# Three passages of a two-block network: where VectorE's low parts and a modulation unit stand, and how many fillers TensorE runs

## The reference, cut to what matters

```python
mod = cond @ ada_w[layer] + ada_b[layer]        # shift1, scale1, gate1, shift2, scale2, gate2
hn = rmsnorm(x, norm1_w[layer]) * (1 + scale1) + shift1
y = mlstm_mixer(hn, ...)  # layer 0;  hgrn2_mixer(hn, ...) in layer 1
x = x + gate1 * y
hn = rmsnorm(x, norm2_w[layer]) * (1 + scale2) + shift2
y = swiglu(hn, ...)       # layer 0;  moe_swiglu(hn, ...) in layer 1, 8 experts, top 2
x = x + gate2 * y
```

## Time and profile before

| | |
|---|---|
| median of three runs | 1492.36 us (1489.75 to 1493.78) |
| profiled execution, its span | 1492.0 us |
| TensorE busy | 1435.4 us, 96% |
| VectorE busy | 1129.3 us, 76% |
| ScalarE busy | 773.8 us, 52% |
| mean granted TensorE clock | 0.989 of full |
| HBM read | 343.65 MB, 231 GB/s over the span |

### The profile page before, as it was taken

The page is one execution under the profiler, slowest core; times in us unless marked ns, Lnnn a source line. Parts: engine busy times, 40 slices in busy tenths (PEclk is TensorE's granted clock), DMA queues, the critical chain, the costliest instruction groups (busy, mean ns, idle before and its releaser), DMA issues.

```text
span 1492.0 us, 21141 instructions
## 1 busy us (share of the span) xinstructions
PE 1435.4 (96%) x8403; PEld 1235.9 (83%) x8403; DVE 1129.3 (76%) x1244; ACT 773.8 (52%) x829; POOL 4.1 (0%) x7
## 2 busy tenths in 40 slices
PE   3998989999999999999999999999999999999999
PEld 3976889799798788878888888787887787899997
DVE  5898578766779866798989889988886767655544
ACT  1535333333455463777777767776565443533332
POOL 0000000000000000000000000000000000000000
PEclk9999899999999999999999999999999999999999
DMA  8877278876865463799999999984554345345652
GB/s 314 274 266 270 64 246 275 301 254 222 271 219 185 148 239 115 255 341 334 333 342 313 362 337 330 352 304 141 175 171 162 113 129 181 114 156 197 198 162 105
DMA packets 198431, 345.83 MB, mean 232 GB/s; under 512 B 11632, under 2 KB 90064, under 8 KB 193232
## 3 DMA queue, kind: packets, MB, share of 16 engines
q1 hardware_dynamic: 190320, 338.71, 66.8%
q10 hardware_dynamic: 8032, 6.01, 1.3%
HBM read 343.65 MB, written 1.05 MB: 231 GB/s over the span
## 4 chain that ended last, share of the span: by engine, by line
PE 51%; DVE 6%; issue 2%; ACT 2%; DVEq 0%; ACTq 0%
PE ps L1313 15%; PE ps L1315 15%; PE ps L1314 15%; DVE wlo L2104 3%; ACT whi L634 1%; PE ps L1372 1%; PE ps L1959 1%; PE ps L1999 1%; DVE HL L2955 0%; PE ps L1982 0%; DVE acc L2945 0%; PE ps L1510 0%; PE ps L1519 0%; PE ps L1518 0%; PE ps L1432 0%
## 5 line engine op out<-in xcount | busy, mean ns | idle before, releaser
L2104 DVE TENSOR_TENSOR wlo<-raw,whi 128x2048 fp32r<-128x2048 f32 (+2 forms) x220 | 480.2, 2193 | 157.3 <-ACT whi L634 151.9
L634 ACT ACTIVATE whi<-raw 128x2048 fp32r<-128x2048 f32 (+2 forms) x220 | 403.8, 1837 | 359.1 <-PE ps L1315 232.8
L1313 PE MATMUL ps<-whi,AH 128*128 128x512 f32 (+1 forms) x816 | 321.4, 394 | 3.7 <-DVE wlo L2104 2.2
L1315 PE MATMUL ps<-whi,AL 128*128 128x512 f32 (+1 forms) x816 | 312.4, 383 | 0.0
L1314 PE MATMUL ps<-wlo,AH 128*128 128x512 f32 (+1 forms) x816 | 312.2, 383 | 0.0
L1313 PE MATMUL ps<-AH,whi 128*128 128x256 f32 x896 | 256.4, 286 | 3.4 <-DVEq L2210 1.4
L1314 PE MATMUL ps<-AL,whi 128*128 128x256 f32 x896 | 254.6, 284 | 0.0
L1315 PE MATMUL ps<-AH,wlo 128*128 128x256 f32 x896 | 254.5, 284 | 0.0
L1313 PEld LDWEIGHTS ps<-whi,AH 128*128 128x128 f32 x816 | 154.0, 189 | 40.9 <-DVE wlo L2104 11.0
L1313 PEld LDWEIGHTS ps<-AH,whi 128*128 128x128 f32 x896 | 173.1, 193 | 5.9 <-issue 2.9
L1315 PEld LDWEIGHTS ps<-whi,AL 128*128 128x128 f32 x816 | 153.7, 188 | 28.2
(11 more groups left out here) (345 smaller groups left out, 1452.1 us busy)
## 6 DMA issues: line engine op xcount, KB each, us to landing
raw<-in_ada_w SPq DMA_DIRECT2D x48, 1024.0 KB, 5.5
raw<-in_w_in SPq DMA_DIRECT2D x26, 1024.0 KB, 5.2
raw<-in_moe_w_up SPq DMA_DIRECT2D x24, 1024.0 KB, 7.0
raw<-in_h_w_in SPq DMA_DIRECT2D x16, 1024.0 KB, 5.8
raw<-in_moe_w_gate SPq DMA_DIRECT2D x16, 1024.0 KB, 7.3
raw<-in_moe_w_down SPq DMA_DIRECT2D x16, 1024.0 KB, 6.5
acc<-in_moe_w_down SPq DMA_DIRECT2D x16, 1024.0 KB, 7.7
raw<-in_m_w_in SPq DMA_DIRECT2D x12, 1024.0 KB, 6.0
```

The lines of the kernel that those rows point to most:

```text
L634: act.activation(whi[:, h, 0:n], raw_at[s][:, 0:n], ACT.Copy).then_inc(w_hi, 1)
L1313: pe.matmul(o, sh, mh, start=first, stop=False)
L1315: return pe.matmul(o, sl, mh, start=False, stop=last)
L2104: dve.tensor_tensor(wlo[:, h, 0:n], raw_at[s][:, 0:n], whi[:, h, 0:n].bitcast(fp), ALU.subtract)\
```

## The change

At passage 1 the first of the next stage's two low parts and the modulation unit go ahead of residual 0, and the second low part goes behind the features. At passage 3 the first low part goes ahead of residual 0, the second behind three small preparations of the router (the last a `memset`), ahead of the wait for the router's product. At passage 2 residual 0 goes ahead of the down product's last low part (only in the second group, `early`), one of the next stage's two low parts stays ahead of residual 1, and one goes behind the features. ScalarE's second high part goes ahead of `first_squares` at passages 1 and 3; at passage 2 the first goes ahead of it and the second stays behind it. Fillers ahead of the transposes: 12 to 11, 16 to 10 and 20 to 11; ahead of the experts: 11 to 3. The order of the loads that SP issues is the same.

```diff
             for j in range(LEAD):
                 hi(w)
                 skip_first(j)
-                if j == 0:
-                    first_squares(0)
+            first_squares(0)
             second_squares(0)
...
+            hi(w)
             first_squares(1)
-            his(w, LEAD)
+            hi(w)
             second_squares(1)
...
-            hi(w)
+            his(w, LEAD)
             first_squares(2)
-            hi(w)
             second_squares(2)
...
-            transposes(w, 12)
+            transposes(w, 11)
...
-            transposes(w, 16)
+            transposes(w, 10)
...
-            transposes(w, 20)
+            transposes(w, 11)
...
-            keep_busy(w, 11)
+            keep_busy(w, 3)
...
-            def out_matrix(w, ahead, tile, units=(2, 4), ready=0):
-
-                first = w.unit - LEAD - ready
-                los(w, 2 - ready)
-                residual(w, 0, first + units[0], GB[:, 0, :], s=x_part)
-                ahead()
-                residual(w, 1, first + units[1], GB[:, 0, :], tile, x_part)
+            def out_matrix(w, first, tile):
+
+                residual(w, 0, first + 3, GB[:, 0, :], s=x_part)
+                residual(w, 1, first + 4, GB[:, 0, :], tile, x_part)
...
-            def group_from(w, first, first_unit, done, side, gate, tile, s, hidden_out):
+            def group_from(w, first, first_unit, done, side, gate, tile, s, hidden_out, early):
 
                 for j in range(first, 18):
+                    if j == 17 and early:
+                        evac_d(w, first_unit, 0, gate, tile, s)
                     lo(w, JOBS[j])
                     side(j)
...
-                evac_d(w, first_unit, 0, gate, tile, s)
+                if not early:
+                    evac_d(w, first_unit, 0, gate, tile, s)
...
-                               (hidden_out, lambda: None)[e])
+                               (hidden_out, lambda: None)[e], e == 1 and not last)
...
                         if not last:
-                            los(w, LEAD)
+                            lo(w)
                         evac_d(w, unit, 1, gate, tiles, s)
...
-            def ffn_start():
-                for j in range(LEAD):
-                    lo(w)
-                    ffn_ada(0, j)
-
-            out_matrix(w, ffn_start, 1, units=(3, 4), ready=2)
+            first_out = w.unit - 4
+            lo(w)
+            ffn_ada(0, 0)
+            out_matrix(w, first_out, 1)
 
             norm_scale(mod[:, 3, :], vec[:, V_NORM2:V_NORM2 + 8])
             normalise(X, True)
             to_features(w, scl, mod[:, 2, :])
+            lo(w)
+            ffn_ada(0, 1)
...
             to_features(w, scl, mod[:, 0, :])
+            lo(w)
...
-            def expert_start():
-                w.depth = N_RAW_E
-                los(w, LEAD)
-
-            out_matrix(w, expert_start, 4, units=(3, 4), ready=2)
+            first_out = w.unit - 4
+            w.depth = N_RAW_E
+            lo(w)
+            out_matrix(w, first_out, 4)
...
             dve.memset(slot_of, 0.0)
+            lo(w)
             dve.wait_ge(small_mm, 2)
```

## The result

The changed kernel takes 1481.24 us in the median of 14 runs (1478.0 to 1487.44), the kernel before 1492.14 us in 14 runs beside it. The ratio is 0.9933, with a 95% interval of 0.9921 to 0.9944: 10 us, or 0.67%, less. Two later measurements of the same kernel gave 0.9920 each. The forecast was 1478.9 us, 13.1 us less, in a range of 1474.0 to 1485.5. The direction and the size hold; the sum was 1 to 3 us too large.

What follows compares the result with a forecast made beforehand. TensorE, 96% busy, was taken as the bound, with passages set by the residual, norm, transposes chain that VectorE started late. Terms 2.5 + 3.6 + 3.8 + 3.2 = 13.1 us off 1492.0 gave 1478.9 us, range 1474.0 to 1485.5.

Steps and rivals of the forecast that it cites:

- What bounded the passages: At the three passages residual, norm and transposes end last, started late by VectorE's order; X 4.0, 3.6, 3.8 us earlier.
- The clock at passage 1: Passage 1's transposes, without idle time before them, run at full clock: another 1.5 us, FFN about 5.5 us earlier.
- The ring behind passage 1: First FFN group: the fourth unit's load, issued at 198.0, waits for a slot, so 2.5 of 5.5 us stay.
- two signs that I named: Transposes begin near 404.9 - 2.5 at passage 2 and near 569.9 - 6.1 at passage 3.
- Passage 2: X whole 3.6 us earlier; the late load slot in the next stage costs nothing, bound 3 us lost.
- Passage 3: X whole at 566.65 instead of 570.49 by the same reordering: 3.8 us; the second low part costs nothing.
- The experts' start: Ahead of the experts, 8 fillers fewer give 3.55 us, less 0.35 for waits: 3.2 us, bounds 2.4 and 3.55.
- The sum: Passages 1 to 3 and the experts' start: 2.5 + 3.6 + 3.8 + 3.2 = 13.1 us less.
- The clock rival: With fewer fillers the clock falls at passages 2, 3 and ahead of the experts: 1484.0 us, chance 0.12.
- Its part ahead of the experts: If the clock falls ahead of the experts, their first 4.2 us take 2.1 us longer.
- The slower rival: Behind passage 1 the late load makes each ring turn 3.5 us longer: 1497.5 us, chance 0.03.
- The rival by which the ring doesn't bind: Loads behind passage 1 catch up, so it keeps its 5.5 us: 16.1 us less, 1475.9 us, chance 0.17.

Runs made afterwards that it cites:

- e7_lo_early: Changed kernel with passage 1's second low part ahead of residual 1 and 12 fillers for 11; ratio 0.9897 to the kernel before, 0.9901 when repeated.
- e2: Changed kernel with passage 2 put back (orders of VectorE and ScalarE, 16 fillers); ratio 0.9954 to the kernel before.
- e5: Kernel before with only the smaller numbers of fillers (11, 10, 11, 3), orders as before; ratio 1.0000 to the kernel before.
- e3: Changed kernel with passage 3 put back (orders of VectorE and ScalarE, 20 fillers); ratio 0.9951 to the kernel before.
- e1: Changed kernel with passage 1 put back (orders of VectorE and ScalarE, 12 fillers); ratio 0.9951 to the kernel before.
- e6_order_only: Changed kernel with the old numbers of fillers (12, 16, 20, 11); ratio 0.9962 to the kernel before.

## Why the prediction was right, and where it wasn't

- **What bounded the passages.** Right. X came 1.61 us behind the product's end at passage 1, as worked out (1.64; tile 1 started 0.20 us behind the fillers' start, estimated at 0.25); 4.0 us of VectorE's order came out there, 3.67 and 3.85 at the others, for 4.0, 3.6 and 3.8 forecast. The transposes start 3.16 us behind X as before.
- **The clock at passage 1.** The 16 transposes take 2.00 us for 3.52, but the start of the FFN moves by 4.74 us, not 5.5. Step that failed: I counted all 1.5 us. The FFN's first product needs the first half of the features only, and so the first eight transposes: from the transposes' start it takes 5.17 us for 5.89, 0.72 less.
- **The ring behind passage 1.** Right in kind: the load was issued at 199.68, which is 198.0 on the clock of before, as forecast, and was used 5.07 us later (5.4 taken). But TensorE didn't stop there. Its first stall of the group stands at 242 us, for 2.11 us, some four turns of the ring later. What the group gives back is 2.0 us in the mean of seven profiles (104.16 us against 102.15 of three with the old order); 4.74 - 2.0 = 2.7 us stay, for 2.5 forecast. That the size agrees is luck: 0.8 too much was counted as won and 1.0 too much as given back, and the 2.0 are uncertain by a us or two. In the first pair of profiles alone nothing was given back. From the FFN's first product to the fillers of passage 2 takes 201.02 us before, in a profile with a stall and half clock of its own, and 199.07 after. So two signs that I named didn't come: passage 2's transposes begin at 399.90, not near 402.4, and passage 3's at 562.49, not near 563.8, although this execution came to passage 1 later by 1.72 us. What I hadn't allowed for is this spread: 4 us between profiles of one kernel in the first group alone. The Trainium skill's rule in "DMA: Bandwidth & Descriptors", "Rules for kernel authors", is to issue a load early and wait for it late. The trace agrees: e7_lo_early follows it, pays 0.54 us for it in the passage, and its two profiles are 3 us shorter in the group behind.
- **Passage 2.** The 3.67 us are there, but I put the late slot in the next stage at nothing, on the strength of one wait for TensorE. In the changed kernel that high part and one ahead of it wait for their loads, and TensorE waits 1.65 us at the second state product, where it was 0.36 before and 0.62 in e2, which has the old order of this passage; the eleven profiles of the new order have 1.08 to 2.13. The rows of SP, ScalarE and TensorE in the changed kernel, and last TensorE's in the kernel before:

```profile
408.69 0.37 SPq L470 DMA_DIRECT2D raw<-in_h_w_in  x1
...
414.20 1.91 ACT L634 ACTIVATE whi<-raw 128x2048 fp32r<-128x2048 f32 x1 [7.43 <-DMA raw<-in_h_w_in]
...
443.39 1.15 PE L1759 MATMUL ps<-acc 128*64 128x64 f32 x32 [1.65 <-DVE acc L2558]
```

```profile
450.75 1.15 PE L1760 MATMUL ps<-acc 128*64 128x64 f32 x32 [0.36 <-DVE acc L2558]
```

  Step that failed: the term put at nothing. About 1 us was given back, within the bound that I had named (3 us) and not in the sum.
- **Passage 3.** Right, 3.85 for 3.8 at the router's start; whether the router stage gives some of it back, the profiles can't tell.
- **The experts' start.** 3.2 forecast, 2.2 measured in the first profile and 2.4 in the mean. Step that failed: I took off 0.35 for waits. TensorE waits for the whole of the experts' input, the case that stood as the lower bound (2.4), and the small transposes that I put between wait with it (1.10 us ahead of line 1524).
- **The sum.** 2.7 + 2.7 + 3.85 + 2.4 = 11.65 us by the profiles, for 13.1 forecast; measured 10 (8 to 12), and 11.9 twice more. The first two terms rest on means over stretches that differ by up to 5 us between single profiles.
- **Rivals.** The clock rival didn't come true in the changed kernel, and came true at passages 2 and 3 where fillers alone were taken (e5): 3.68 us for 16 transposes. Its part ahead of the experts came true nowhere, and the 4.2 us taken for it are the length of the window in the earlier trace rows; TensorE ran at half clock there for 6.8 us. The Trainium skill's "HAM oscillation" in "TensorE: Matmul & The Clock Gate" has the clock throttled again when TensorE waits between bursts. The trace of e5 agrees: the granted clock was 0.50 after 5.10 and 3.71 us of waiting. X early enough is what kept the changed kernel from it. The slower rival asked for 2.5 us a turn of the ring; the group became 2 us longer in all. The rival by which the ring doesn't bind fits the first pair of profiles, and only the means and e7_lo_early speak against it.

## What to carry to other kernels

When TensorE runs fillers, look for what they wait for, move work that isn't part of that chain out of it, and take the fillers away afterwards and with it: here the order alone was worth 5.7 us, the fillers alone nothing, and both 10 to 12. A step that frees a buffer for a load has a second due date besides that of its reader. Before it is moved behind a chain, ask when the load that waits for it will then go out; a place half a microsecond dearer in the chain can be the cheaper one.

## What the hardware showed besides

Behind one and the same wait of TensorE the granted clock fell in some executions and held in others. Near 1000 to 1014 us, in a stage that the change doesn't touch, TensorE waits for VectorE's queue in all of these kernels. First the kernel before, its row and its window over the 4 us behind (columns as above):

```profile
1014.48 0.47 PE L1518 MATMUL ps<-z_back 128*128 128x512 f32 x1 [2.79 <-DVEq L2966]
```

```profile
1014.50:1018.50 4.00, 4.00 (x18) 3.29 (x19) 3.95 (x4) 0.83 (x1) 0.00 (x0) 1.00 0.00 0
```

Then the changed kernel:

```profile
1002.83 0.47 PE L1517 MATMUL ps<-z_back 128*128 128x512 f32 x1 [2.79 <-DVEq L2966]
```

```profile
1002.90:1006.90 4.00, 4.00 (x11) 3.15 (x12) 3.40 (x4) 0.79 (x1) 0.00 (x0) 0.57 0.01 4
```

The idle time is 2.79 us in both; the clock stays at 1.00 in one and is 0.57 in the other, with 11 matmuls done for 18. Of 14 profiles 3 kept the clock here (before, e2, e3), and the old and the new orders stand on both sides, so it isn't the change's doing. A fall costs 1 to 2 us, and some 5 in the longest stretch (10 us, in the router stage), if half of the time at half clock is counted as lost, an estimate. Without the one at the very end a profile has five to nine of them. All 14 have one near 40 us, between 140 and 151, between 169 and 175 and between 564 and 583; the others differ between profiles of one kernel.

After 3.45 us without a matmul (before, e1) or more (e5) the clock had fallen at each of these passages; after 1.37 us it hadn't. Between these, waits of like length went either way. First e1_no_p1, at 0.50 from 442.9 us on, then e6_order_only, at 1.00 from 252.4 to 258.0 us:

```profile
442.73 1.93 PE L1760 MATMUL ps<-acc 128*64 128x64 f32 x32 [1.84 <-DVE acc L2559]
```

```profile
252.30 0.39 PE L1312 MATMUL ps<-AH,whi 128*128 128x256 f32 x1 [2.12 <-DVE wlo L2103]
```
